# A four-layer decoder on one core: each engine gets an order of its own in the mixer stages, and the first kind of layer closes its mixing by token tile

## What is computed

```python
# first kind, per layer
h = rms_norm(x, pre_mix_g[l]); z = h @ w_in[l]
o_a = hgrn2_mixer(...); o_b = gla_mixer(...)        # gated linear attention, A and B
o_c = mla_mixer(...)                                # causal softmax attention, C
o_d = gdn_mixer(...)                                # gated delta rule in chunks of 64, D
x = x + rms_norm(concatenate([o_a, o_b, o_c, o_d]) @ w_out[l], post_mix_g[l])
h = rms_norm(x, pre_ffn_g[l]); x = x + rms_norm(conv_glu_ffn(h, ...), post_ffn_g[l])
# second kind, per layer
h = rmsnorm(x, g_pre_mix); proj = h @ w_in
# a: top-k selected attention, b: forgetting, c: differential, d: sliding window with sinks
x = x + rmsnorm(concatenate([o_a, o_b, o_c, o_d]) @ w_out, g_post_mix)
m = square(relu(rmsnorm(x, g_pre_mlp) @ w_up)) @ w_down; x = x + rmsnorm(m, g_post_mlp)
x = x + sigmoid(x @ w_ple_gate) * (p_i @ w_ple_proj)
```

## Time and profile before

| | us |
|---|---|
| median of 3 runs | 1838.51 |
| lowest and highest | 1835.78, 1843.68 |
| profiled execution | 1842.62 |
| its span, first to last instruction | 1840.8 |
| PE busy | 1697.9 (92%) |
| DVE busy | 988.4 (54%) |
| ACT busy | 695.0 (38%) |
| mean granted clock of TensorE | 0.941 |

### The profile page before, as it was taken

How to read it: one execution, slowest core, us unless ns; L and a number is a source line. 1 busy time by engine, 2 the same in 40 slices (tenths; PEclk the granted TensorE clock), 3 DMA queues, 4 the chain that set the end, 5 groups by cost and what they waited for, 6 DMA issues and landing times.

```text
span 1840.8 us, 28182 instructions
## 1 busy us (share of the span) xinstructions
PE 1697.9 (92%) x11516; PEld 1481.2 (80%) x11516; DVE 988.4 (54%) x1515; ACT 695.0 (38%) x1147; POOL 0.2 (0%) x4
## 2 busy tenths in 40 slices
PE   7999987999999988799999987899999989799998
PEld 7877567998887756699888775899889777599887
DVE  3254656775334466577742656466452275456545
ACT  2222435444313143534441234555353125445434
POOL 0000000000000000000000000000000000000000
PEclk9989897999998989799999988899999889889999
DMA  9310014555640100365555300355547411236553
GB/s 330 88 44 25 1 40 155 182 193 189 206 142 24 47 1 24 117 215 175 201 183 161 92 23 24 131 173 197 197 160 213 114 47 46 92 115 186 192 192 106
DMA packets 186242, 232.15 MB, mean 126 GB/s; under 512 B 22497, under 2 KB 161537, under 8 KB 185985
## 3 DMA queue, kind: packets, MB, share of 16 engines
q1 hardware_dynamic: 186112, 230.34, 38.7%
HBM read 229.28 MB, written 1.05 MB: 125 GB/s over the span
## 4 chain that ended last, share of the span: by engine, by line
PE 84%; DVE 7%; ACT 4%; DVEq 2%; issue 1%; DMA 1%; ACTq 1%; SPq 0%
PE banks L421 83%; DVE all_ring_rounded L2668 1%; ACT all_ring_rounded L2487 1%; DMA all_ring<-in_w_ple_gate 1%; DVE all_work L2734 0%; ACT all_rest L2491 0%; PE banks L2169 0%; ACT all_ring_rounded L1312 0%; ACT all_work L2499 0%; DVE all_work L2771 0%; DVE all_work L2730 0%; ACT all_rest L347 0%; DVE x_state L386 0%; PE banks L897 0%; DVEq L2770 0%
## 5 line engine op out<-in xcount | busy, mean ns | idle before, releaser
L421 PE MATMUL banks<-all_mix_rounded,all_ring_rounded 128*128 128x256 f32 (+1 forms) x2496 | 466.3, 289 | 10.9 <-DVEq L417 10.9
L421 PE MATMUL banks<-all_ring_rounded,all_work_rounded 128*128 128x512 f32 (+1 forms) x1728 | 430.4, 387 | 29.8 <-DVEq L2689 21.1
L421 PEld LDWEIGHTS banks<-all_mix_rounded,all_ring_rounded 128*128 128x128 f32 x2496 | 402.7, 198 | 13.9 <-DVEq L417 11.9
L421 PEld LDWEIGHTS banks<-all_ring_rounded,all_work_rounded 128*128 128x128 f32 x1728 | 327.4, 191 | 96.1 <-DVEq L2689 21.9
L421 PE MATMUL banks<-all_work,all_ring 128*128 128x256 f32 (+3 forms) x1856 | 357.2, 355 | 16.0 <-DVEq L406 6.0
L421 PE MATMUL banks<-all_work_rounded,all_ring_rounded 128*128 128x256 f32 (+1 forms) x1248 | 360.3, 289 | 0.0
L421 PEld LDWEIGHTS banks<-all_work,all_ring 128*128 128x128 f32 (+2 forms) x1856 | 307.9, 198 | 60.8 <-issue 16.0
L2668 DVE TENSOR_TENSOR all_ring_rounded<-all_ring,all_ring_rounded 128x2048 fp32r<-128x2048 f32 x82 | 187.9, 2293 | 139.5 <-ACT all_ring_rounded L2487 138.5
L421 PEld LDWEIGHTS banks<-all_work_rounded,all_ring_rounded 128*128 128x128 f32 x1248 | 247.3, 198 | 0.1
L1555 DVE TENSOR_TENSOR all_ring_rounded<-all_ring,all_ring_rounded 128x2048 fp32r<-128x2048 f32 x74 | 169.4, 2292 | 86.1 <-ACT all_ring_rounded L1312 84.7
L421 PE MATMUL banks<-all_work 64*64 64x64 f32 (+8 forms) x2080 | 176.5, 275 | 24.5 <-ACT all_work L2491 7.4
(11 more groups left out here) (256 smaller groups left out, 1262.9 us busy)
## 6 DMA issues: line engine op xcount, KB each, us to landing
all_ring<-in_w_in SPq DMA_DIRECT2D x48, 1024.0 KB, 6.0
all_ring<-in_w_mlp_up SPq DMA_DIRECT2D x32, 1024.0 KB, 5.4
all_ring<-in_w_mlp_down SPq DMA_DIRECT2D x32, 1024.0 KB, 4.9
all_ring<-in_ffn_w_gate SPq DMA_DIRECT2D x22, 1024.0 KB, 5.2
all_ring<-in_ffn_w_up SPq DMA_DIRECT2D x22, 1024.0 KB, 5.5
all_ring<-in_ffn_w_down SPq DMA_DIRECT2D x22, 1024.0 KB, 5.0
all_ring<-in_w_out SPq DMA_DIRECT2D x12, 1024.0 KB, 5.1
all_ring<-in_w_ple_gate SPq DMA_DIRECT2D x8, 1024.0 KB, 5.3
```

Of the source, the lines that this page charges most:

```text
L421: ins = self.nc.tensor.matmul(out, lhsT, rhs, start=start, stop=stop)
```

## The change

`interleave` and the one list go. Each kind of layer gets three lists, `ORDER["PE"]`, `ORDER["ACT"]` and `ORDER["DVE"]`, written out as text that `in_order` expands (`in:8` is eight steps of `in`), and `turns_in` takes the list of the engine that signals. In the first kind C's transposes, values and split are made per token tile (steps 7 to 10 on each engine, banks `c_o0` and `c_o1`); the output projection is taken in three parts, `early` (tiles of A and D), `rest` (B) and `late` (C), with `late` by token tile, and its panels are cut to match: `out0` and `out1` hold the tiles 0, 1, 6, 7 in two DMAs each, `out2` and `out3` the tiles 2 to 5. In the closing `gate_up` takes the gate and up matmuls of the first two column tiles (`AHEAD` = 2) over the first 128 tokens before the second tile is ready and over the second 128 afterwards; ACT and DVE finish token tile 0, `gate0` and `up0` before they start on token tile 1. In the second kind only the lists change, and `select` gets one more drain.

```diff
-    late = [(f"1{layer}.out{2 * half + n}", wout(512 * half, 512 * half + 512)[:, 4 * n:4 * n + 4, :], 4, 0, 512) for half in range(2) for n in range(2)]
+    def rows_of(half, n):
+        w = wout(512 * half, 512 * half + 512)
+        return w[:, 2:6, :] if n else [(slice(0, 2), ALL, w[:, 0:2, :]), (slice(2, 4), ALL, w[:, 6:8, :])]
+
+    late = [(f"1{layer}.out{2 * n + half}", rows_of(half, n), 4, 0, 512) for n in range(2) for half in range(2)]
...
-    HASTE = 0.94
     LEVEL_STEPS = len(LEVELS) + 3
-    GLA_STEPS, MLA_STEPS, GDN_STEPS = 3 + LEVEL_STEPS + 3, 10, 29
-    others = (interleave(["A"] * (GLA_STEPS - 2), ["in"] * 10) + ["A", "B", "A", "mix"]
-              + interleave(interleave(["B"] * (GLA_STEPS - 1), ["C"] * 4), ["out"] * 5))
-    ORDER = (["in"] * 10 + ["D"] + ["in"] * 7 + ["D", "in"] + interleave(["D"] * (GDN_STEPS - 2), others, HASTE)
-             + ["mix"] + interleave(["C"] * (MLA_STEPS - 4), ["early"] * 4) + ["mix"])
-    made, squared = (turns_in(ORDER, {"A": ("A", LEVEL_STEPS + n), "B": ("B", LEVEL_STEPS + n), "D": ("D", GDN_STEPS - 6 + n)}) for n in (3, 4))
+    GLA_STEPS, MLA_STEPS, GDN_STEPS = 3 + LEVEL_STEPS + 3, 11, 29
+    ORDER = {
+        "PE": in_order("""
+            in:8 D in:9 D in A:2 D in D in A:2 D in D A in D:2 A:2 in D out A D in A D A in D:2 out A in out A D in A D
+            A D in D A D A out B A D mix D B D B D C B:2 out D B C D B:3 C D B D B D B C D B:2 D B C B:2 early C early:2
+            rest C:2 rest mix early C:2 late C rest:2 late"""),
+        "ACT": in_order("""
+            in:9 D in:8 D in A D in A D in A:2 D in D A in D:2 A:2 in D A D in A out A D in D:2 out A in D out A in A D
+            A D:2 A D in A B out A D mix D B D B C D out B:2 D B C D B C D B D B:2 D B:2 C D B:2 D B C B:2 early C rest
+            early:2 C:2 rest mix C:2 late early C rest late rest"""),
+        "DVE": in_order("""
+            in:9 D in:8 D in A D A in A D in D A in D in A D A D A in D A D out in A D A in D:2 A out in A out D in D
+            A:2 in D:2 A D A B out A D mix D B D B D C B out B D B C D B:2 C B D:2 B:2 D B C D B:2 D B C B early B
+            early:2 C mix C rest C:2 rest C late C rest early rest late"""),
+    }
+    made, squared = (turns_in(ORDER[engine], {"A": ("A", LEVEL_STEPS + n), "B": ("B", LEVEL_STEPS + n), "D": ("D", GDN_STEPS - 6 + n)})
+                     for engine, n in (("DVE", 3), ("ACT", 4)))
+    split_off = turns_in(ORDER["DVE"], {"A": ("mix", 0), "B": ("mix", 1), "D": ("D", GDN_STEPS - 1), "C0": ("C", 8), "C1": ("C", 10)})
 
 
     FIRST = 3
+    AHEAD = 2
...
-            yield
-            pe.wait_ge(*due("PT", 3))
-            pe.wait_ge(*due("mla_v", 1))
...
+                yield
+                pe.wait_ge(*due("PT", 2 * t + 1))
+                pe.wait_ge(*due("mla_v", 1))
+                b = psum.claim(pe, f"c_o{t}")
+                for h in range(4):
+                    o, v = shaped(b[:, 0:T], 2, P)[HD * (h % 2):HD * (h % 2) + HD, h // 2], slice(HD * h, HD * h + HD)
+                    for kt in range(t + 1):
+                        last = mm(o, vtokC[:, kt, v], PT[t, kt][:, h, :], not kt, kt == t)
+                last.then_inc(psum.full_of(f"c_o{t}"), 1)
+                yield
...
+        PARTS = {"early": (0, 1, 6, 7), "rest": (2, 3), "late": (4, 5)}
+        PLACE = {tile: (n, k) for n, tiles in enumerate(((0, 1, 6, 7), (2, 3, 4, 5))) for k, tile in enumerate(tiles)}
 
         def mix(t, half, tiles):
 
             b = psum.bank(f"mix{half}{t}")
-            for k in tiles:
-                panel = f"out{2 * half + k // 4}"
+            for tile in tiles:
+                n, k = PLACE[tile]
+                panel = f"out{2 * n + half}"
                 w = kit.split_panel(pe, ring, panel)
-                last = mm3(b[:, :], [a[:, k, t * P:(t + 1) * P] for a in (rounded(hT), rounded(mixT))], [a[:, k % 4, :] for a in w], k == 0, k == 5)
-                if k in (3, 5) and t == NT - 1:
+                last = mm3(b[:, :], [a[:, tile, t * P:(t + 1) * P] for a in (rounded(hT), rounded(mixT))], [a[:, k, :] for a in w], tile == 0, tile == 5)
+                if tile in (5, 7) and t == NT - 1:
                     kit.free_panel(ring, panel)
             return last
 
         def mix_early():
             mixed.extend(psum.hold(4))
-            pe.wait_ge(*due("mix_split", 3))
+            pe.wait_ge(*due("mix_split", max(split_off["A"], split_off["D"])))
             for t in range(NT):
                 for half in range(2):
                     psum.claim(pe, f"mix{half}{t}", mixed[2 * t + half])
-                    mix(t, half, (0, 1, 2, 3, 6, 7))
+                    mix(t, half, PARTS["early"])
                     yield
 
+        def mix_rest():
+            pe.wait_ge(*due("mix_split", split_off["B"]))
+            for t in range(NT):
+                for half in range(2):
+                    mix(t, half, PARTS["rest"])
+                    yield
+
+        def mix_late():
+            for t in range(NT):
+                pe.wait_ge(*due("mix_split", split_off[f"C{t}"]))
+                for half in range(2):
+                    mix(t, half, PARTS["late"]).then_inc(psum.full_of(f"mix{half}{t}"), 1)
+                yield
+
+        emit(ORDER["PE"], {"in": project(), "A": gla(G["A"], 0), "B": gla(G["B"], 1), "C": mla(), "D": gdn(), "out": iter(range(5)), "mix": iter(range(2)),
+                     "early": mix_early(), "rest": mix_rest(), "late": mix_late()})
+        psum.let_go(mixed[0:2])
+        kit.give_back(pe)
+        h = (rounded(mixT), rounded(hT))
+
+        def gate_up(j, half, tokens):
+
+            w = kit.split_panel(pe, ring, f"{('gate', 'up')[half]}{j // 2}")
+            c, b = (j % 2) * P, psum.bank(f"ff{j}")
+            for k in range(KT):
+                last = mm3(b[:, half * T + tokens.start:half * T + tokens.stop], [a[:, k, c:c + P] for a in w],
+                           [a[:, k, tokens] for a in h], k == 0, k == KT - 1)
+            if j % 2 and tokens.stop == T:
+                kit.free_panel(ring, f"{('gate', 'up')[half]}{j // 2}")
+            return last
+
+        kit.normed_transposes(pe, psum, "hT1", 2 * layer + 1, 0)
+        pe.wait_ge(kit.sems["h_split"], NT * layer + 1)
+        for half in range(2):
+            for j in range(AHEAD):
+                if not half:
+                    psum.claim(pe, f"ff{j}")
+                gate_up(j, half, slice(0, P))
+            if not half:
+                kit.normed_transposes(pe, psum, "hT1", 2 * layer + 1, 1)
+        psum.let_go(mixed[2:4])
+        pe.wait_ge(kit.sems["h_split"], NT * layer + 2)
+        for j in range(FT):
+            if j >= AHEAD:
+                psum.claim(pe, f"ff{j}")
             for half in range(2):
-                mix(t, half, (4, 5)).then_inc(psum.full_of(f"mix{half}{t}"), 1)
-        psum.let_go(mixed)
-        kit.give_back(pe)
+                last = gate_up(j, half, slice(P, T) if j < AHEAD else slice(0, T))
             last.then_inc(psum.full_of(f"ff{j}"), 1)
-            if j % 2:
-                kit.free_panel(ring, name)
...
         kit.exp_and_ln()
         names = [[f"mix{half}{t}" for half in range(2)] for t in range(NT)]
         kit.statistics_of_y(act, psum, 2 * layer, 0, names[0])
+        round_weights("gate0")
         kit.statistics_of_x(act, 2 * layer + 1, 0, kit.x_halves(2 * layer, 0))
-        round_weights("gate0")
-        kit.statistics_of_y(act, psum, 2 * layer, 1, names[1])
         kit.upper_half_of_hT(act, psum, "hT1", 0, PAR("pre_ffn"))
         kit.round_upper_half(act, 0)
+        round_weights("up0")
+        kit.statistics_of_y(act, psum, 2 * layer, 1, names[1])
         kit.statistics_of_x(act, 2 * layer + 1, 1, kit.x_halves(2 * layer, 1))
-        round_weights("up0")
         kit.upper_half_of_hT(act, psum, "hT1", 1, PAR("pre_ffn"))
         kit.round_upper_half(act, 1)
...
         kit.gained(dve, psum, 2 * layer, 0, names[0], gain_rows, yn)
         kit.added(dve, psum, 2 * layer, 0, names[0], yn)
         kit.scale_rows(dve, 2 * layer + 1, 0)
         subtract_rounded("gate0")
+        kit.lower_half_of_hT(dve, psum, "hT1", 0, PAR("pre_ffn"))
+        kit.split_h(dve, layer, 0)
+        subtract_rounded("up0")
         kit.gained(dve, psum, 2 * layer, 1, names[1], gain_rows, yn)
-        kit.lower_half_of_hT(dve, psum, "hT1", 0, PAR("pre_ffn"))
         kit.added(dve, psum, 2 * layer, 1, names[1], yn)
-        kit.split_h(dve, layer, 0)
         kit.scale_rows(dve, 2 * layer + 1, 1)
         kit.lower_half_of_hT(dve, psum, "hT1", 1, PAR("pre_ffn"))
         kit.split_h(dve, layer, 1)
-        subtract_rounded("up0")
...
-    ORDER = """
-        in in in in in in in index in in index c forget select in c select in c forget c in forget b c in b c out c in b c b in c
-        a b out c in b a b a in b a out in a a p a in d a d out split split split early d early d d rest rest d late early early d
-        d rest rest late
-        """.split()
+    ORDER = {
```

(20 more changed lines are left out.)

80 lines of the change are left out of this document (23 added, 57 removed).

## The result

The changed kernel takes 1789.8 us (median of 4, 1783.1 to 1791.1), the kernel before 1837.1 in the same comparison: ratio 0.9725, 95% interval 0.9701 to 0.9748. A second comparison on another chip gave 0.9728 (0.9715 to 0.9741). That is 50 us less; I had predicted 22. The direction was right and the time lies in the range, but the gain was more than twice my number.

What follows compares the result with a forecast made beforehand. PE idle time in mixer stages and lost clock were taken to bound the kernel. First-kind layers +19.5 - 13 = +6.5, second-kind -17.7, two of each: -22.4, so 1820 us as profiled, 1816 against the median; range 1777 to 1848.

Steps and rivals of the forecast that it cites:

- What bounds the kernel: Mixer stages: PE waits on an order of steps, not a full engine; an idle us removed is a us of span.
- What would show it: Signs: 10.4 us wait gone, mixing idle about 8, closing idle about 4, 128x128 matmuls at clock 0.50 for some 45 us.
- Part 1: Second-kind layers: new orders save 17.7 us a layer: 9 split wait, 5 mid-stage, 1.5 small waits, 2.2 clock.
- Part 2: First kind's mixing: new orders save 13 us a layer, 9 of idle time and 4 of clock.
- Part 3: First kind's closing by token tile: costs 19.5 us more a layer, bounds 0 and 22.
- 1.2 GHz through all of it: New closing: after a 3.1 us gap, 192 matmuls of 128 columns and transposes all run at half clock.
- The walk: New closing timed step by step at half clock from the mixing's end M: 128-column matmuls end at M + 50.2.
- rival B: First kind's closing: clock is up, by holding over the gap or dense transposes; closing costs 0, 1777 us; chance 0.19.
- C's new waits: Mixing: new orders bring waits, such as for PSUM banks, 1 to 3 us each; 1860 us; chance 0.14.
- D: Orders gain half (6.5 and 10 a layer), closing costs as forecast; about 1842 us, no change; chance 0.17.

Runs made afterwards that it cites:

- second_kind_only: The kernel before with only the second kind's three lists and the drain in the selection changed: 1803.7 us, ratio 0.9813.
- mixing_only_first_kind: The kernel before with the first kind's lists and mixing by token tile, but the old closing and old second kind: 1807.9 us, ratio 0.9823.
- old_closing: The changed kernel with the first kind's closing put back: both transposes, then gate and up over 256 tokens, old ACT and DVE order there: 1780.9 us, ratio 0.9673.
- transposes_last: The changed kernel with the second tile's transposes behind all 96 gate and up matmuls of the first 128 tokens: 1822.4 us, ratio 0.9899.
- splits_moved_ahead: The kernel before with the first two split steps moved ahead of d's score steps and out3 in the second kind's one list: 1834.3 us, ratio 0.9964.
- spare_transposes: transposes_last plus two groups of 16 unread fp32 matmuls of the transposes' form among the closing's 128-column matmuls: 1816.4 us in a single execution.

## Why the prediction was off, point by point

- **What bounds the kernel.** Right. PE idle time in the mixer stages was the cost, and a us of it removed was a us of the span: the 55 us of idle removed carry the whole gain.
- **What would show it.** The 10.4 us wait went, and the closing's idle time is 3.4 us (I had about 4). Mixing idle is 10.2 and 10.1, where I had about 8 for both. The row of matmuls 128x128 is there, but the clock is at 0.50 for 10.2 us, 3.8 of them transposes, and not for 45.
- **Part 1, second kind (17.7 us a layer).** Right in sum: mixing lost 17.2, second_kind_only 18. By terms it was 12.4 us of idle, not 15.5, and 4.8 of clock, not 2.2: 9.5 of the idle time at `early` (I had 9), and 3 in all the rest (I had 6.5), since a wait of 2.2 us on a bank is new there. My 9 us for the moved splits hold only with PE's and ACT's new places too; the move alone gave about 3 a layer, since d's probabilities are late next. The prediction said what is late next but counted on the three `early` steps that the new list puts there.
- **Part 2, first kind's mixing (13).** Direction right, size low: 16.7 by mixing_only_first_kind. Idle 7.5 a layer against my 9; clock 9 against my 4. Some 3 us of the 16.7 lie not in the mixing at all but in the closing behind it, by `late` in two token tiles: the same closing work ends at M + 32.5 in before and at M + 29.5 in old_closing, 0.9 of it less idle time (10.97 us against 11.9) and the rest clock, which in before was at 0.50 from 276.9 to 297.3 and in old_closing for 10 us in two stretches. Where the rest of the clock's 9 us lies was not traced.
- **Part 3, the closing (19.5 more a layer).** The failed step is "1.2 GHz through all of it". The walk's events were right: the idle time (3.1 forecast, 2.73 seen), the gate matmuls and then dense transposes at half speed (but for the first 22 matmuls), and no further gap. The clock was not. By the trace the new closing ends 1.4 us later than the old one did in before (M + 33.9 against the M + 32.5 worked out from rows of before), and 4.4 later than the old closing does behind the new mixing. For the two closings I had +39; the runs have +9 and +10. That difference, 29 us, is as large as the whole miss (1820 forecast for the profiled run, 1791.1 seen); the smaller errors of the other terms (8 us) and the 10 us by which the parts overshoot the whole cancel. The prediction also has a slip of 1 us: 96 matmuls that become 192 cost 192 x 0.110 - 96 x 0.119 = 9.7 us more at full clock, not 10.7; the walk doesn't use it.
- **Why that step was wrong.** From 10.0 us of matmuls of 128 columns at 0.50 I concluded that matmuls of this width run slow. The row shows only that they do not raise the clock. The row next to it, 5.3 us of the same matmuls at 1.00, shows that for so long they do not lower it either, and I used it for rival B alone. What happens is then decided by what else stands in the stretch, and there stood the transposes: in before 3.78 us of them had run at half clock and been followed by a gap, so no row showed them in unbroken work. I named the case in rival B ("or the dense transposes lift it") and gave it 0.19.
- **The Trainium skill's rule** (TensorE: Matmul & The Clock Gate, What's actually happening: slow is the default and activity releases it) was nearer to the outcome than my reading, since the closing came out as rival B has it. But not for every kind of work: in transposes_last 20.5 us of unbroken matmuls of 128 columns did not release it, twice in a closing.
- **Rivals.** B (1777) was nearest: its mechanism is the one that occurred, with 10.2 us of half clock left. Of C's new waits little came: 2.2 us on a bank (L2840), and in the first kind the longest wait is 3.0 us, on ACT's copies of `w` (L1524), where before had 0.5. The trace of before could not show how the banks would turn, so that these stayed small is luck in part. D did not occur as a whole; its first half, that part of the orders' gain returns as other waits, is what splits_moved_ahead shows for one edit alone. Its time doesn't come out of its sum: 1838.5 + 6 is 1844, not 1842.

## What to carry to other kernels

Ask of each kind of matmul three things of the clock, not one: whether a stretch of it raises it, holds it or lets it fall; a row at 0.50 answers only the first. Before cutting work by tokens to fill a gap, compare the time of the half-width matmul with the full one; where they are nearly equal, shorten the chain that makes the gap instead (here the old closing, with either order on ACT and DVE, did better than 96 matmuls a layer cut into 192). And when a wait of 10 us is removed, look at PE's own order behind it: without that, over half of it came back at the next step.

## What the runs showed of the chip

- In unbroken work PE's clock rose to full speed within or just behind a run of fp32 matmuls of 128 columns (at 281.5 in after, where they stand from 277.07 to 280.9; at 278.8 in spare_transposes, where they begin at 274.48), and not in 20.5 us of fp32r matmuls of 128 columns. In transposes_last those of 256 columns raised it after 3.8 us. With idle time on both sides, 3.8 us of the fp32 ones raised it in old_closing and not in before.
- Once up, it held at 1.00 over 15.7 us of those same fp32r matmuls. It fell behind the gaps of 2.73 us that stood ahead of them: 2.6 us into them in after, 0.5 us in transposes_last (292.62, down at 293.1).
- Idle time of the two parts of the change added up (24.7 + 30.3 = 55.0), and it differed by 0.7 us between two profiles of one kernel (87.9 and 87.2). PE's busy time does not hold as still: five executions of old_closing have spans of 1770.8 to 1783.2 us with granted clocks of 0.967 to 0.958. So a difference of 10 us in busy time between two single profiles is within the scatter.
